# Turned probabilities in pieces of 2, 4 and 3 tiles, rotations without the gates' store, and earlier weight loads in a two-block transformer

## The reference, cut to what matters

```python
for l in range(DEPTH):                          # DEPTH = 2, L = 1040
    u = rms_norm(h, norm_w[l]) @ w_in[l]
    f_in, f_gate, p_in, p_gate, c_q, c_kv, k_r, a_gate = jnp.split(u, split_idx, axis=-1)
    y_f = fourier_mix(f_in, fourier_w[l]); y_p = pool_mix(p_in, pool_w[l], pool_scale[l])
    y_a = mla_mix(c_q, c_kv, k_r, q_norm_w[l], w_uq[l], kv_norm_w[l], w_ukv[l], cos, sin)
    mix = jnp.concatenate([y_f * jax.nn.silu(f_gate), y_p * jax.nn.silu(p_gate),
                           y_a * jax.nn.silu(a_gate)], axis=-1)
    h = h + mix @ w_out[l]

# mla_mix, 4 heads: q and k have 128 columns from a normalized latent and 64 rotated ones
q = (rms_norm(c_q, q_norm_w) @ w_uq)            # last 64 columns of a head: apply_rope
kv = (rms_norm(c_kv, kv_norm_w) @ w_ukv)        # k_nope and v; k_rope = apply_rope(k_r)
s = jnp.einsum('bqhd,bkhd->bhqk', qb, k) * 192 ** -0.5
p = jax.nn.softmax(s, axis=-1)
o = jnp.einsum('bhqk,bkhd->bqhd', p, v)
```

## Time and profile before

| | |
|---|---|
| median of 3 runs | 3832.7 us (3831.67 to 3835.75) |
| the profiled execution | 3843.3 us, its span 3841.5 us |
| TensorE busy | 3668.5 us, 95% of the span |
| VectorE, ScalarE, GpSimd busy | 1678.4, 1258.8, 1084.7 us |
| granted TensorE clock, mean | 0.984 |
| attention of the second block, first layer | about 2896 to 3150 us |
| changes of layer | about 1320, 2600 and 3225 us |

### The profile page before, as it was taken

How to read it: one execution, slowest core, us unless ns; L and a number is a source line. 1 busy time by engine, 2 the same in 40 slices (tenths; PEclk the granted TensorE clock), 3 DMA queues, 4 the chain that set the end, 5 groups by cost and what they waited for, 6 DMA issues and landing times.

```text
span 3841.5 us, 50299 instructions
## 1 busy us (share of the span) xinstructions
PE 3668.5 (95%) x20446; PEld 3234.5 (84%) x20446; DVE 1678.4 (44%) x3146; ACT 1258.8 (33%) x2869; POOL 1084.7 (28%) x794
## 2 busy tenths in 40 slices
PE   6999998999999999999999999999999999999998
PEld 5887887878887788888878888888999999999998
DVE  5434555333344453255534333455344435434433
ACT  3112444033342121044422333323235532224541
POOL 3633222321212354323322212124530113531012
PEclk9999999999999999999999999999999999999999
DMA  3122111411014311201022111241110012111012
GB/s 112 44 69 72 34 37 51 145 44 39 31 39 156 104 66 50 88 31 47 31 102 88 44 45 39 108 146 60 57 57 14 26 61 99 63 50 33 16 44 100
DMA packets 85190, 243.81 MB, mean 63 GB/s; under 512 B 10720, under 2 KB 24800, under 8 KB 84960
## 3 DMA queue, kind: packets, MB, share of 16 engines
q1 hardware_dynamic: 84960, 240.61, 18.5%
HBM read 190.04 MB, written 50.53 MB: 63 GB/s over the span
## 4 chain that ended last, share of the span: by engine, by line
PE 74%; DVE 12%; ACT 8%; issue 4%; POOL 1%; DMA 1%; SPq 0%; DVEq 0%; POOLq 0%; ACTq 0%
PE pj L1460 29%; PE pS L1460 24%; PE po L1691 4%; PE po L1583 4%; PE pS L1671 3%; PE pS L1673 2%; DVE tmp L2336 2%; DVE KK L2348 1%; PE pS L1554 1%; DVE tmp L2339 1%; PE pS L1555 1%; ACT PT L1899 1%; PE pt L1570 1%; DVE tmp L2333 1%; ACT P L1890 1%
## 5 line engine op out<-in xcount | busy, mean ns | idle before, releaser
L2779 POOL TENSOR_SCALAR Whi<-stage 128x1024 fp32r<-128x1024 f32 (+3 forms) x252 | 260.0, 1032 | 1970.6 <-DMA stage<-wstream 1273.2
L1460 PE MATMUL pj<-Hhi,Whi 128*128 128x512 f32 x1640 | 663.3, 404 | 9.4 <-DVE Hlo L2201 2.9
L1460 PE MATMUL pj<-Hhi,Wlo 128*128 128x512 f32 x1640 | 646.1, 394 | 0.0
L1460 PE MATMUL pj<-Hlo,Whi 128*128 128x512 f32 x1640 | 645.0, 393 | 0.0
L2781 POOL TENSOR_TENSOR Wlo<-stage,Whi 128x1024 fp32r<-128x1024 f32 (+3 forms) x252 | 593.7, 2356 | 21.0
L1460 PEld LDWEIGHTS pj<-Hhi,Whi 128*128 128x128 f32 x1640 | 312.7, 191 | 80.5 <-ACT PT L1899 6.6
L1460 PEld LDWEIGHTS pj<-Hhi,Wlo 128*128 128x128 f32 x1640 | 311.5, 190 | 67.5
L1460 PEld LDWEIGHTS pj<-Hlo,Whi 128*128 128x128 f32 x1640 | 312.4, 190 | 59.8
L1460 PE MATMUL pS<-Hhi,Whi 128*128 128x512 f32 x792 | 315.5, 398 | 17.5 <-DVE Hlo L2201 9.6
L1460 PE MATMUL pS<-Hlo,Whi 128*128 128x512 f32 x792 | 313.5, 396 | 0.0
L1460 PE MATMUL pS<-Hhi,Wlo 128*128 128x512 f32 x792 | 313.2, 396 | 0.0
(11 more groups left out here) (462 smaller groups left out, 7624.7 us busy)
## 6 DMA issues: line engine op xcount, KB each, us to landing
stage<-wstream SPq DMA_DIRECT2D x228, 512.0 KB, 4.3
merged<-Mb SPq DMA_DIRECT2D x32, 512.0 KB, 2.9
Mb<-merged SPq DMA_DIRECT2D x32, 512.0 KB, 4.4
gates<-tmp SPq DMA_DIRECT2D x48, 256.0 KB, 2.2
TH<-gates SPq DMA_DIRECT2D x24, 512.0 KB, 5.8
xres<-X SPq DMA_DIRECT2D x16, 520.0 KB, 2.9
xr<-xres SPq DMA_DIRECT2D x16, 520.0 KB, 4.4
X<-xT SPq DMA_DIRECT2D x16, 256.0 KB, 6.9
```

The costliest lines, as they stand in the source:

```text
L1460: x = pe.e.matmul(ps, w[a][:, v.koff + k * P:v.koff + k * P + P], moving(v.of, b, k, v.t0, v.n), start=k == 0 and i == 0, stop=k == v.K - ...
L2779: pool.e.tensor_scalar(upper, stage, 1.0, 0.0, ALU.mult, ALU.add).then_inc(*pool.tick("whi", c))
```

## The change

There are three parts.

**Pieces.** The nine turned tiles of a step go in pieces of 2, 4 and 3: tiles 0 and 1 to `pt`, 2 to 5 to one bank of `pj`, 6 to 8 to another. ScalarE copies the first two pieces. VectorE copies the third in two instructions, since tile 8 has 112 rows and the others 116. `values2` takes tiles 0 and 1, `values2_rest` 2 to 5 and 6 to 8. The scores of a step wait bank by bank: banks 0 and 1 for `exp2a`, bank 2 for `exp2`.

**Stores.** `latent` keeps the two last gate stores in `self.stored` and no longer in `self.ph`. The rotations, queries and keys of `attention2` don't wait for them. `values_in` and what follows do. No instruction moves by it on any engine.

**Loads.** Load c stands at `behind[split[c - 2]]`, behind the place where the stage's former content is split. The list `split` holds the places of the splits, which stay as they were.

```diff
+PIECES = [(0, 2), (2, 4), (6, 3)]
...
-        at = 0
+        at, split = 0, []
         for c in range(len(self.weights)):
             b = self.before[c]
-            free = self.first[c].id if c < NR else self.split_at.get(c, 0) if b is None else behind[self.used_at[b]]
-            at = max(at, self.sent.get(c, free))
+            free = self.split[c].id if c < NR else self.split_at.get(c, 0) if b is None else behind[self.used_at[b]]
+            at = max(at, self.first[c].id if c < NR else self.sent.get(c, behind[split[c - NS]]))
+            split.append(max([free, self.split_at.get(c, 0)] + split[-1:]))
             self.units[at].setdefault("loads", []).append(c)
-            self.units[self.split[c].id if c < NR else max(at, free, self.split_at.get(c, 0))].setdefault("splits", []).append(c)
+            self.units[split[c]].setdefault("splits", []).append(c)
...
         self.run(gate(3))
         self.phase()
-        self.ph = self.ph + stored
+        self.stored = stored
...
-        self.run(kv[2:] + v[0:3])
+        self.run(kv[2:])
+
+        self.ph = self.ph + self.stored
+        for u in v:
+            u["ph"] = self.ph
+        self.run(v[0:3])
...
             softened[s] = u
-            self.scores_free = [("exp2", u.id)]
+            self.scores_free = [("exp2a", u.id), ("exp2a", u.id), ("exp2", u.id)]
 
         def turns(s):
             pieces = []
             u = self.put("turns2", **geometry(s), soft=softened[s].id, pieces=pieces, pt_free=pt_free[0])
-            for f in range(0, 9, 4):
+            for f, n in PIECES:
                 if f == 0:
-                    pieces.append((f, None, self.pt_free))
+                    pieces.append((f, n, None, self.pt_free))
                     self.pt_free = ("pt2_out", u.id, f)
                 else:
                     b, free = self.take()
-                    pieces.append((f, b, free))
-                    self.bank_free[b] = ("pt2_out", u.id, f) if f < 8 else ("pt2_last", u.id)
-            p_free[s % 2] = ("p2_turned", u.id, 8)
+                    pieces.append((f, n, b, free))
+                    self.bank_free[b] = ("pt2_out", u.id, f) if f < 6 else ("pt2_last", u.id)
+            p_free[s % 2] = ("p2_turned", u.id, 6)
...
-        self.bank_free[2:5], self.banks = self.scores_free * 3, WIDE
+        self.bank_free[2:5], self.banks = self.scores_free, WIDE
...
     def scores2(u):
-        for x in u.free + u.ready:
+        for x in u.ready:
             pe.wait_ge(x)
         qs, q, r = slice(u.q0, u.q0 + u.nq), m.qn, m.qr[(0, 1, 0, 2)[u.h]]
         for c, (t0, n) in enumerate(TS2):
+            pe.wait_ge(u.free[c])
...
     def turns2(u):
         nq = u.nq
-        for f, b, free in u.pieces:
+        for f, count, b, free in u.pieces:
             pe.wait_ge(("exp2", u.soft))
             pe.wait_ge(free)
             bank = m.pt if b is None else m.pj[b]
-            for i, (t0, n) in enumerate(KT[f:f + 4]):
+            for i, (t0, n) in enumerate(KT[f:f + count]):
...
     def pv(u, f):
-        pe.wait_ge(("pt2_out", u.turns, f) if f < 8 else ("pt2_last", u.turns))
+        pe.wait_ge(("pt2_out", u.turns, f) if f < 6 else ("pt2_last", u.turns))
...
-        for i, (t0, n) in list(enumerate(KT))[f:f + 4]:
+        for i, (t0, n) in list(enumerate(KT))[f:f + dict(PIECES)[f]]:
...
     def values2_rest(u):
-        for f in (4, 8):
+        for f in (2, 6):
             pv(u, f).then_inc(*pe.tick("values2", u.id, f))
...
     def turns2(u):
-        for f, b, free in u.pieces:
-            if f == 8:
-                return
-            src = (m.pt if b is None else m.pj[b])[0:116, 0:512].rearrange("p (a b) -> p a b", a=4)[:, :, 0:u.nq]
+        for f, n, b, free in u.pieces[0:2]:
+            src = (m.pt if b is None else m.pj[b])[0:116, 0:n * P].rearrange("p (a b) -> p a b", a=n)[:, :, 0:u.nq]
...
-            act.e.activation(m.PT2[u.l][0:116, f:f + 4, 0:u.nq], src, ACT.Copy).then_inc(*act.tick("pt2_out", u.id, f))
+            act.e.activation(m.PT2[u.l][0:116, f:f + n, 0:u.nq], src, ACT.Copy).then_inc(*act.tick("pt2_out", u.id, f))
...
     def turned_last(u):
         bank = m.pj[u.bank]
-        n = KT[8][1]
-        dve.wait_ge(("p2_turned", u.of, 8))
+        dve.wait_ge(("p2_turned", u.of, 6))
         dve.wait_ge(u.pt_free)
         phase_met(u)
-        dve.e.tensor_copy(m.PT2[u.l][0:n, 8:9, 0:u.nq], bank[0:n, 0:P].rearrange("p (a b) -> p a b", a=1)[:, :, 0:u.nq]).then_inc(
-            *dve.tick("pt2_last", u.of))
+        for a, b, n in ((6, 8, KT[7][1]), (8, 9, KT[8][1])):
+            src = bank[0:n, (a - 6) * P:(b - 6) * P].rearrange("p (a b) -> p a b", a=b - a)[:, :, 0:u.nq]
+            dve.e.tensor_copy(m.PT2[u.l][0:n, a:b, 0:u.nq], src).then_inc(*dve.tick("pt2_last", u.of))
```

More of the change, by code:

```diff
@@ L1330, in attention2 @@
                 soft(s + 1)
-            self.put("turned_last", of=turned[s].id, bank=turned[s].pieces[-1][1], pt_free=pt_free[0], **geometry(s))
+            self.put("turned_last", of=turned[s].id, bank=turned[s].pieces[-1][2], pt_free=pt_free[0], **geometry(s))
             if q == nt - 2 and h < 3:
```

## The result

The changed kernel takes 3807.9 us, median of 4 runs (3806.7 to 3810.4), against 3834.2 us for the kernel before, timed beside it. The ratio is 0.9933, with a 95% interval of 0.9915 to 0.9950: faster by 26 us, between 19 and 33. A second measurement gave 0.9917 (0.9904 to 0.9930), 32 us. The forecast was 3802, with a range of 3789 to 3821.

The account below looks back on a forecast made before the run. TensorE, busy for 95% of the span, bounds the kernel, so only its waits can be saved: 21 (pieces) + 3.3 (stores) + 7 (loads) = 31 us off the 3832.7 median gives 3802 us, range 3789 to 3821.

Parts of the forecast that it names:

- The first part, 21 us: Second block's attentions: smaller first copy and scores released by bank end TensorE's waits, 21 us, range 12 to 21.
- The margin of the second copy: Attention step: the four-tile second copy is ready for its reader with 0.06 us to spare, the change's tightest margin.
- The rival of the second copy: Attention steps: second copy becomes the new wait, 49 steps lose 0.1 us each, loads bring nothing; 3816 us, chance 0.13.
- the fourth rival: Attention: TensorE's gap belongs to something else, such as switching from transposes to values, so pieces don't matter; 3822 us, chance 0.10.
- The extra waits of the scores: Added semaphore waits on 68 score groups: 0 to 0.08 us each, taken as 0, with 5 us kept for the range.
- The second part, 3.3 us: Second block's rotations no longer wait for the gates' store: 1.7 us in one layer, 1.6 in the other, range 1.6 to 4.
- The third part, 7 us: Three layer changes: earlier weight loads remove waits for weights, 4.5 us, and one collision, 2.2; range -3 to 16.
- one collision less: Second block's first layer change: one of two VectorE subtractions stretched by a GpSimd split goes, saving 2.2 us.
- third rival's price of a hit: Earlier splits landing on VectorE operations TensorE waits for cost 2.2 us per hit; slower-kernel rival, chance 0.04.
- the queue's price: SyncE's queue: nothing already due stands behind an early load, so 0; at worst one split on an unawaited store.
- The third rival's count: 11 net new hits eat the first two parts' gain; 16 of some 250 splits make it 3844 us, chance 0.04.
- The clock: Layer changes: TensorE's granted clock is 0.74; up to 6 us may return with shorter waits, none taken.

Follow-up runs that it names:

- e7_one: The changed kernel with pieces of 1, 4 and 4 instead of 2, 4 and 3: 3815.0 us, ratio 0.9952 to the kernel before.
- e10_whole: The changed kernel itself with all three parts, timed once more: ratio 0.9917 to the kernel before, -31.8 us.
- e1_pieces: The kernel before with the first part alone, pieces of 2, 4 and 3 and scores released bank by bank: ratio 0.9941, -22.6 us.
- e3_loads: The kernel before with the third part alone, the earlier weight loads: ratio 1.0002, +0.8 us.
- e2_stores: The kernel before with the second part alone, rotations not waiting for the gates' store: ratio 0.9994, -2.3 us.
- e9_two: The kernel before with the first and second parts, without the earlier loads: ratio 0.9936, -24.6 us.
- e8_behind: Changed kernel with the third output weight's split held for VectorE's last low half, and merge weight loads behind the gates' loads: 3799.7 us, ratio 0.9910.
- e5_banks: The kernel before with only the scores released bank by bank, pieces left at 4, 4 and 1: ratio 0.9992, -3.1 us.

## Why the prediction was right, step by step

- **The first part, 21 us.** 22.6 timed, 21.2 in the trace. The step's working held nearly to the hundredth: ScalarE's copy of 232 columns 0.36, VectorE's 0.39, values right behind the transposes, second reader without idle. By layer the working gives 26 x 0.32 + 6 x 0.40 = 10.7 and 23 x 0.30 + 6 x 0.40 = 9.3, and the values' spans shrank by 10.5 and 9.0. The margin of the second copy, put at 0.06, was 0.04: the copy ends at 2905.95, 0.05 go to hand it over (as in e7_one, 2909.75 to 2909.80), and the reader starts at 2906.04. And e7_one shows that the worry was right: with one tile of values less ahead of its reader the copy is waited for. The rival of the second copy would have been true one tile further on. The idle in rows 4 was the copy's, not the switch to the values, which was the fourth rival.
- **Instructions of fewer columns.** The copies by ScalarE took 0.27, 0.36, 0.46 and 0.56 for 116, 232, 348 and 464 columns. So some 0.17 of each is there whatever its size. The Trainium skill (VectorE: DVE Perf Modes, on the TRN2 errata) gives ScalarE a fixed part of 172 cycles at 1.2 GHz for reads of PSUM, an estimate of 0.14 us; the trace has slightly more. Its advice of tiles of at least 512 elements stands there for operations that read SBUF, which these copies don't, and the engine that pays the fixed part has time here.
- **The extra waits of the scores** cost nothing that the steps show, as taken.
- **The second part, 3.3 us.** 2.3 timed, 2.2 in the stretches. The rotations start after 0.97 us of idle, behind their projection, and not after 2.6, as expected; a third of the gain doesn't reach the scores.
- **The third part, 7 us.** This is the term that was mis-sized, and the step that failed is the one that put the price at 0: that SyncE has nothing behind an early load that is already due, and that splits only land badly by chance. The gains came where they were expected. The waits for low weights are 4.6 less in the trace after and 3.6 in e10_whole (4.5 foreseen); at the first change in the second block the wait of 5.7 became two of 1.7 and 1.9, 2.1 less, as for one collision less (2.2 foreseen). In time, 9.8 us at the changes of layer, of which 3.3 went again behind the second. But in the last merges the load waits for a split still running, with the gate's load behind it, and the stage that now lies ready lets the next split start the moment that TensorE leaves the slot, which is when VectorE makes the last two inputs of the output projection. That cost 10.4 us, 12.5 against the undisturbed executions. Holding the split gave 5.3 of it back, 2.2 and 3.1 at the two places, and moving the loads behind the gates' gave the rest. So the third rival's price of a hit, 2.2 us, was about right; the queue's price, put at 0, was the other half.
- **The third rival's count.** Over the whole trace, VectorE's operations that took over 1.2 us longer than their like are 61 before, 62 in e1_pieces, 71 in e3_loads and 73 after. The net new hits that the rival needed, 11, did come, and my argument against it, that hits would move both ways, failed. What kept the kernel from losing is that most of them landed where TensorE doesn't wait: its list of waits shows a price for two.
- **The clock.** I took none of the possible 6 us. At the changes of layer some came back (by the brackets 11.9 before and 5.1 after, but 3.4 more behind the second), and at the merges 5.1 were lost.

The sum was 31, and the two measurements say 26 and 32. Without the third part's gain the first two give 25, so the forecast held because its largest term was read from a steady pattern, and because the part that failed was small: its 7 us are about what 3802 missed the first measurement by, 6. The second measurement lies 1 us beside the forecast, but the stretches together show no net gain of the third part, so that is no confirmation of its 7.

## What to carry to other kernels

Where the bound engine turns tiles and reads them back through another engine's copy, make the first copy small enough to end when the last tile is turned, and check the second copy in the same way; a step's start times give both to 0.05 us. A transfer that comes earlier is not free even when its queue looks idle: ask which wait it carries past the others, and what the work behind it will start earlier and run over. A late DMA can be what keeps two engines out of each other's way, and when it goes, its ordering has to be written down as a wait.

## What the runs showed of the hardware

- A VectorE operation with two inputs from SBUF and GpSimd's passes over a weight exclude each other nearly whole: 2.83 us for the low half under the second pass and 0.68 alone, 1.29 and 0.69 for the addition under the first. Each ended 0.54 to 0.55 us behind the end of GpSimd's pass (1224.39 and 1223.85, 1227.15 and 1226.60). The Trainium skill (SBUF — State Buffer, Who interferes with whom) says that the later one waits for the whole other instruction, and the trace agrees.
- The lower clock level does not follow from the length of the last idle alone. Ahead of the first layer's output projection, idle of 2.2 us left the clock at the upper level in five executions, and idle of 4.0 and 6.5 us was followed by 6.8 us at the lower one, the first matmul at 0.77 us instead of 0.47. At the same place in the second layer, idle of the same 2.2 us was followed by 3.4 us at the lower level in the kernel before, e1_pieces, e2_stores, e9_two and e8_behind, and by none in e5_banks. Single profiled executions of one kernel differ by it: 108 and 125 us at the lower level in after and e10_whole, whose spans are 3808.3 and 3812.2 us.
